# Prompt attention with part of the scaling on GpSimd, masks in fp32r, keys split in two parts, and two gathers moved by one stage

## The reference, cut to what matters

```python
N_HEADS, N_KV_HEADS, HEAD_DIM = 8, 2, 64       # 4 query heads to each key head
o_c, imp = cmp_attend(q, ckv, pos)             # 16 compressed keys, from compress(kvc)
idx, valid = select_blocks(imp, pos)           # 16 blocks of 64 keys: with 1024 keys, all of them
o_s = sel_prompt(q_rot, pos, idx, valid, kvs)  # so this is causal attention over all earlier keys
o_w = window_prompt(q_rot, kvw)                # the last 512 keys, by another set of keys and values
attn = g[:, :, 0] * o_c + g[:, :, 1] * o_s + g[:, :, 2] * o_w   # gates, per position and head
```

## Time and profile before

| | us |
|---|---|
| median of 3 runs | 1815.67 (1811.49 to 1818.6) |
| the profiled execution | 1816.98 |
| its span in the profile | 1814.5 |
| stage of keys ends, compression begins | at 379.3 |
| prompt attention, 128 steps | 529.8 to 815.5, its first maximum at 544.0 |

### The profile page before, as it was taken

How to read it: one execution, slowest core, us unless ns; L and a number is a source line. 1 busy time by engine, 2 the same in 40 slices (tenths; PEclk the granted TensorE clock), 3 DMA queues, 4 the chain that set the end, 5 groups by cost and what they waited for, 6 DMA issues and landing times. The chain is left out here.

```text
span 1814.5 us, 29420 instructions
## 1 busy us (share of the span) xinstructions
PE 1686.8 (93%) x11053; PEld 1490.5 (82%) x11053; DVE 949.3 (52%) x1625; ACT 756.4 (42%) x1233; POOL 340.3 (19%) x360
## 2 busy tenths in 40 slices
PE   6999979969979998998779999999999999999997
PEld 3888955558866777775569999999999999999997
DVE  3747672234457787774466644443444443444443
ACT  3435511124446576672233555432345332354322
POOL 1100051511020010021036404004213023100032
PEclk7999989978878999997889999999999999999999
DMA  8355320063502000104544444534544545445343
GB/s 298 106 151 173 102 75 24 0 222 125 179 5 93 2 1 1 53 2 198 235 121 131 128 139 133 145 112 129 154 134 139 150 123 156 141 134 161 113 141 96
DMA packets 296946, 214.36 MB, mean 118 GB/s; under 512 B 20293, under 2 KB 284277, under 8 KB 293590
## 3 DMA queue, kind: packets, MB, share of 16 engines
q1 hardware_dynamic: 290340, 176.51, 32.8%
q0 software_dynamic: 4672, 36.56, 5.3%
q10 hardware_dynamic: 1842, 0.05, 0.1%
HBM read 205.81 MB, written 11.41 MB: 120 GB/s over the span
## 5 line engine op out<-in xcount | busy, mean ns | idle before, releaser
L423 DVE TENSOR_TENSOR ff_lo<-ff_raw,ff_hi 128x2048 fp32r<-128x2048 f32 (+1 forms) x126 | 267.2, 2121 | 201.3 <-ACT ff_hi L419 201.2
L428 PE MATMUL banks<-low_rows,ff_hi 128*128 128x352 f32 x1120 | 359.2, 321 | 0.0
L427 PE MATMUL banks<-ff_h_hi,ff_hi 128*128 128x352 f32 x1056 | 341.7, 324 | 1.0 <-DVE ff_lo L423 0.9
L429 PE MATMUL banks<-ff_h_hi,ff_lo 128*128 128x352 f32 x1056 | 339.1, 321 | 0.0
L419 ACT ACTIVATE ff_hi<-ff_raw 128x2048 fp32r<-128x2048 f32 (+1 forms) x126 | 215.4, 1710 | 229.7 <-PE banks L429 220.0
L428 PEld LDWEIGHTS banks<-low_rows,ff_hi 128*128 128x128 f32 x1120 | 210.8, 188 | 0.3
L427 PEld LDWEIGHTS banks<-ff_h_hi,ff_hi 128*128 128x128 f32 x1056 | 198.1, 188 | 2.0 <-issue 1.8
L429 PEld LDWEIGHTS banks<-ff_h_hi,ff_lo 128*128 128x128 f32 x1056 | 198.2, 188 | 0.0
L427 PE MATMUL banks<-hid_hi,ff_hi 128*128 128x352 f32 x528 | 171.2, 324 | 4.3 <-DVE hid_lo L423 4.1
L429 PE MATMUL banks<-hid_hi,ff_lo 128*128 128x352 f32 x528 | 169.8, 322 | 0.0
L428 PE MATMUL banks<-hid_lo,ff_hi 128*128 128x352 f32 x528 | 169.4, 321 | 0.0
(11 more groups left out here) (435 smaller groups left out, 3231.3 us busy)
## 6 DMA issues: line engine op xcount, KB each, us to landing
ff_raw<-in_w_gate SPq DMA_DIRECT2D x66, 512.0 KB, 3.8
ff_raw<-in_w_up SPq DMA_DIRECT2D x66, 512.0 KB, 5.1
ff_raw<-in_w_down SPq DMA_DIRECT2D x48, 384.0 KB, 3.9
late_ada<-in_w_ada SPq DMA_DIRECT2D x16, 1024.0 KB, 5.5
ff_raw<-in_w_down SPq DMA_DIRECT2D x48, 320.0 KB, 3.2
ff_raw<-in_w_out SPq DMA_DIRECT2D x24, 512.0 KB, 4.5
s_raw<-in_w_in SPq DMA_DIRECT2D x48, 128.0 KB
streams<-in_x_prompt SPq DMA_DIRECT2D x4, 1024.0 KB, 9.2
```

The lines of the kernel that those rows point to most:

```text
L423: return dve.tensor_tensor(lo, raw, hi.bitcast(F32), ALU.subtract)
L427: pe.matmul(out, lhsT=w_hi, rhs=x_hi, start=first, stop=False)
L428: pe.matmul(out, lhsT=w_hi, rhs=x_lo, start=False, stop=False)
L429: return pe.matmul(out, lhsT=w_lo, rhs=x_hi, start=False, stop=last)
```

## The change

1. Stage of keys: POOL issues two gathers (part 0) before its last pair instead of four; those of part 1 are issued by POOL at the start of the stage of compression.
2. Weighing of branch 2 (64 of 128 steps) is shared: DVE makes the reciprocal only and counts `coef_ready`; POOL multiplies by reciprocal and gate. Semaphore `scaled` becomes `scaled_v` and `scaled_p`. POOL's other work in the stage (copies for `q_plain` and `q_rot`, squares) stands between these products.
3. Masks and the identity beside them are fp32r instead of bf16.
4. The first split of keys covers 2 tiles of 8 (256 of 1024 keys); the rest is split by ACT behind the first doubling of queries, and by DVE in round 1. PE waits for the rest before step 8.
5. Half of `q_lo` is cleared by POOL instead of DVE, and PE starts the compressed scores of trip 0 before it waits for the masks.

```diff
@@ keys_and_values, gpsimd
                         pool.wait_ge(nat_summed, T9)
-                        for n in range(2):
-                            for half in range(SG):
-                                load_past(pool, d, hT[:, :, :].rearrange("p k r -> p (k r)"), page_rows, half, n, rows_loaded)
+                        for half in range(SG):
+                            load_past(pool, d, hT[:, :, :].rearrange("p k r -> p (k r)"), page_rows, half, 0, rows_loaded)
@@ compress, gpsimd
-            for n in range(2, N_LCH):
-                pool.wait_ge(multiplied, (n - 1) * STEPS + AHEAD)
+            for n in range(1, N_LCH):
+                if n >= 2:
+                    pool.wait_ge(multiplied, (n - 1) * STEPS + AHEAD)
@@ prompt_attention
+    HEAD_TILES, REST_AT = 2, 1
+    KEY_PARTS = [slice(0, HEAD_TILES * P), slice(HEAD_TILES * P, SEQ)]
-        diag_b, tail_b, ident_b = [sb(nc, st, n, [P, P], mybir.dt.bfloat16) for n in ("diag_b", "tail_b", "ident_b")]
+        diag_b, tail_b, ident_b = [sb(nc, st, n, [P, P], F32R) for n in ("diag_r", "tail_r", "ident_r")]
+        def wait_scaled(eng, n):
+            _, _, br, h = order[n]
+            eng.wait_ge(scaled_v if br == 1 else scaled_p, n // 4 * 2 + h + 1)
@@ gpsimd
+            for h in range(N_KV):
+                pool.memset(QL[h][own[1 - h], :].bitcast(F32), 0.0).then_inc(q_clear, 1)
+                pool.wait_ge(q_clear, h + 1)
             pool.memset(vx, 0.0).then_inc(v_clear, 1)
...
+            steps = spread()
+            for n in range(N + 12):
+                if n < N and order[n][2] == 2:
+                    w, j = len(tiles_of[n]) * P, slice(n % 4, n % 4 + 1)
+                    pool.wait_ge(coef_ready, n // 4 * 2 + order[n][3] + 1)
+                    pool.tensor_scalar(probs[n % 3][:, 0:w], probs[n % 3][:, 0:w], coef[:, j],
+                                       gsel[order[n][0] % 2][:, order[n][1], 2, order[n][3]:order[n][3] + 1], ALU.mult, ALU.mult).then_inc(scaled_p, 1)
+                    pool.wait_ge(scaled_p, n // 4 * 2 + order[n][3] + 1)
+                if n >= 10 and n % 4 == 2 and (n - 10) // 4 // TILES in (1, KA - 1):
+                    square((n - 10) // 4)
+                if n < PER:
+                    next(steps, None)
@@ tensor
             def qk(n):
+                if n == HEAD_TILES * PER // TILES:
+                    pe.wait_ge(k_lo_done, 2 * N_KV)
...
             def turn(n):
-                pe.wait_ge(scaled, n + 1)
+                wait_scaled(pe, n)
...
+            pe.wait_ge(ck_ready, 1)
+            compress_scores(0)
             pe.wait_ge(masks_cast, 3)
-            compress_scores(0)
+            pe.wait_ge(q_clear, N_KV)
@@ scalar
-            for h in range(N_KV):
-                split_hi(act, KS[h][own[h], :, :], kT[own[h], :, 0:SEQ]).then_inc(k_hi_done, 1)
-            double(0, 0)
+            for part in KEY_PARTS:
+                for h in range(N_KV):
+                    split_hi(act, KS[h][own[h], :, part], kT[own[h], :, part]).then_inc(k_hi_done, 1)
+                if part is KEY_PARTS[0]:
+                    double(0, 0)
@@ vector, weigh(n)
-                s.then(dve.reciprocal(coef[:, j], den[:, j]))
-                dve.tensor_scalar(probs[n % 3][:, 0:w], probs[n % 3][:, 0:w], coef[:, j], gsel[i % 2][:, t, br, h:h + 1],
-                                  ALU.mult, ALU.mult).then_inc(scaled, 1)
+                if br == 2:
+                    if n >= 4:
+                        wait_scaled(dve, n - 4)
+                    dve.reciprocal(coef[:, j], den[:, j]).then_inc(coef_ready, 1)
+                else:
+                    s.then(dve.reciprocal(coef[:, j], den[:, j]))
+                    dve.tensor_scalar(probs[n % 3][:, 0:w], probs[n % 3][:, 0:w], coef[:, j], gsel[i % 2][:, t, br, h:h + 1],
+                                      ALU.mult, ALU.mult).then_inc(scaled_v, 1)
@@ vector, the rounds
+                if n == REST_AT:
+                    split_keys(1)
```

More of the change, by code:

```diff
@@ L1359, in prompt_attention @@
         acc = take_space(SEQ)
+        sq = take_space(P)
         diag, tail = probs[0][:, 0:P], probs[0][:, P:2 * P]
@@ L1429, in _, with spread @@
-            s.fence()
-            s = Steps(pool, pool_stepped)
[L1432 to L1443, removed]
-                            r.then_inc(squared, 1)
-                            pool.wait_ge(squared, t + 1)
-                        else:
-                            s.then(r)
+            def spread():
+                s = Steps(pool, queries_spread)
+                s.then(pool.memset(q_plain[:, :, :], 0.0))
+                s.then(pool.memset(q_rot[:, :, :], 0.0))
+                for b in range(BT):
+                    for h in range(N_KV):
+                        part = slice(h * HEAD_DIM, (h + 1) * HEAD_DIM)
+                        c0 = b * QR + h * DEC_SEQ * GROUP
+                        for dst, src in ((q_plain, qT), (q_rot, qR)):
+                            for g in range(SG):
+                                row = SEQ + (g * BT + b) * DEC_SEQ
+                                s.then(pool.tensor_copy(
+                                    dst[part, g * BT + b, c0:c0 + DEC_SEQ * GROUP].rearrange("p (s g) -> p s g", g=GROUP),
+                                    src[part, :, row:row + DEC_SEQ].rearrange("p g s -> p s g")))
+                                yield
@@ new lines, in _, with square @@
+            s = Steps(pool, pool_stepped)
+            def square(tile):
+                i, t = tile // TILES, tile % TILES
+                pool.wait_ge(taken, (tile + 1) * N_KV)
+                rows = slice(t * P, (t + 1) * P)
+                for n, c in enumerate((i // 2, 2 + i // 2)):
+                    x = attnT[:, c, rows]
+                    if i == 1 and n == 0:
+                        s.then(pool.tensor_tensor(acc[:, rows], x, x, ALU.mult))
+                        continue
+                    s.then(pool.tensor_tensor(sq[:, :], x, x, ALU.mult))
+                    r = pool.tensor_tensor(acc[:, rows], acc[:, rows], sq[:, :], ALU.add)
+                    if i == KA - 1 and n:
+                        r.then_inc(squared, 1)
+                        pool.wait_ge(squared, t + 1)
+                    else:
+                        s.then(r)
@@ L1449, in _ @@
+            for _ in steps:
+                pass
+            pool.wait_ge(scaled_p, N // 2)
         @block.tensor
@@ L1685, in weigh, with split_keys @@
                 dve.wait_ge(probs_ready, n + 1)
[L1686 to L1688 removed]
+                if br == 2:
+                    if n >= 4:
+                        wait_scaled(dve, n - 4)
+                    dve.reciprocal(coef[:, j], den[:, j]).then_inc(coef_ready, 1)
+                else:
+                    s.then(dve.reciprocal(coef[:, j], den[:, j]))
+                    dve.tensor_scalar(probs[n % 3][:, 0:w], probs[n % 3][:, 0:w], coef[:, j], gsel[i % 2][:, t, br, h:h + 1],
+                                      ALU.mult, ALU.mult).then_inc(scaled_v, 1)
             s.then(dve.memset(ck_pair[:, :, :], 0.0))
             for h in range(N_KV):
[L1692 removed]
                 s.done(dve.tensor_scalar(ck_pair[own[h], h, :], ck_p[own[h], :], SCALE, None, ALU.mult))
             s.fence()
+            dve.sem_inc(ck_ready, 1)
+            stage(0, 0)
+            def split_keys(part):
+                for h in range(N_KV):
+                    dve.wait_ge(k_hi_done, part * N_KV + h + 1)
+                    keys = KEY_PARTS[part]
+                    split_lo(dve, KS[h][own[1 - h], :, keys], kT[own[h], :, keys], KS[h][own[h], :, keys]).then_inc(k_lo_done, 1)
+            split_keys(0)
             dve.wait_ge(masks_loaded, 48)
@@ L1697, in _ @@
                 dve.tensor_copy(dst[:, :], src[:, :]).then_inc(masks_cast, 1)
-            stage(0, 0)
-            for h in range(N_KV):
-                dve.wait_ge(k_hi_done, h + 1)
-                split_lo(dve, KS[h][own[1 - h], :, :], kT[own[h], :, 0:SEQ], KS[h][own[h], :, :]).then_inc(k_lo_done, 1)
             compress_shift(0)
```

22 lines of the change are left out of this document (4 added, 18 removed).

## The result

The changed kernel took 1793.2 us (1792.1 to 1795.7, 4 runs) beside 1813.9 us of the kernel before on the same chip: ratio 0.9885, 95% interval 0.986 to 0.991. Run a second time beside others it took 1795.4 us, ratio 0.990 (0.988 to 0.992).

A forecast was written before the change was run, and what follows sets the result against it. TensorE was taken to bound most of prompt attention, with DVE next; the terms -5.3 - 1.5 - 4 - 2 + 1.5 + 1 + 3.5 summed to -6.8 us, giving 1809 us, the forecast's own range 1803 to 1815.

The forecast's parts named there:

- gathers: End of the stage of keys: it waits for four gathers to land; issuing two instead saves 5.3 us.
- start: Start of prompt attention: fewer fills and a shorter first split on DVE gain 1.5 us at the maximum at 552.85.
- branch 2 off DVE, t = 5 to 7: Tiles bound by PE: without DVE's product the copy of bank 5 comes earlier and PE's waits end, 4 us less.
- tiles t = 1: Tiles t = 1 of trips 0 to 2, bounded by DVE: three products leave it in each, 2 of 3.3 us gained.
- POOL: DVE's products, L1627: POOL's products hold DVE's own product and, in tiles t = 4 of trips 0 to 2, DVE's L1627: 1.5 us lost.
- POOL: squares: Trips 1 and 3: four squares between a tile's two POOL products make the second late in small tiles, 1 us lost.
- masks fp32r: 160 mask matmuls on PE: 0.04 us more each, 6.4 us, just over half on the path, 3.5 us lost.
- I take 1.9: POOL's product by two columns on 128x640, shown in no row: 1.2 or 2.1 us by proportion, taken as 1.9 us.
- A: Rival, chance 0.23: POOL's product takes 1.2 us so nothing collides, and masks cost nothing; 1803 us, range 1797 to 1807.
- B: Rival, chance 0.12: fp32r masks of 128 columns take 0.22 us, all on PE's path; 1829 us, or 1825.
- C: Rival, chance 0.13: POOL becomes the bound in trips 1 and 3 and blocks DVE; 1820 us.
- D: Rival, chance 0.05: the stage of keys doesn't end on the gathers, or the moved ones are waited for; 1814 us.

The follow-up runs named there:

- pool_twice: The changed kernel with each of POOL's 64 products done twice, the same piece first multiplied by 1 and 1 in place: 1802.2 us, ratio 0.993.

## Why the prediction was wrong

By its terms, in us; measured in the traces where rows give it:

```
term                              forecast (bounds)      measured
gathers                           -5.3 (-6.5..-4.8)      -5.0, -5.8
start                             -1.5 (-4..+1)          -3.0
branch 2 off DVE, t = 5 to 7      -4   (-6.4..-3.1)      -5.8 (6.2 less 0.4 of the masks)
tiles t = 1                       -2   (-3.3..0)         -1.6
POOL: DVE's products, L1627       +1.5 (-2..+5)          none seen in the tiles
POOL: squares                     +1   (0..+7)           0
masks fp32r                       +3.5 (0..+24)          -0.65
sum                               -6.8                   -16 to -17
```

**The failed step** is the side of costs. I put 6 us against the gains for masks and POOL; they cost nothing, and the masks even gained 0.65. For the masks "just over half on the path: 3.5 us" was drawn from a transpose's 0.11 us between starts, the wrong neighbour: the fp32r mask's distance to the next matmul is 0.13 us at 765.88 above, where the bf16 mask had 0.12 in the earlier trace rows. My lower bound of 0 excluded the gain without a reason. For POOL "I take 1.9" lay above the truth by a factor of two, and 0.89 lies below both of my ends (1.2 and 2.1). The slope is (894 - 453) / 512 = 0.86 ns a column. (The Trainium skill's "roughly line-rate", GPSIMD Engine Reference, section 4.1, would have been a better guide than the one-column product of the earlier trace rows.) pool_twice shows that with 1.75 us a loss would have come, in the small tiles with squares and in the tiles t = 4 that I named.

**The gains** were mis-sized the other way. The split keys gave 3.0 and not 1.5. I had the first maximum 2.5 us earlier and 1 us of that lost again to the rest of the split in round 1; it came 3.1 earlier and 0.1 was lost, since VectorE had idled for as long as the rest of the split takes (3.45 beside 3.54 us). In the large tiles I read the earlier trace rows alone. The direction and the mechanism were right (the product before the copy, "this wait of 0.26 us ends"), but the 6.4 us of PE's row were not all: the weight loads waited 13.6 us for the copy and 5.7 for the product, and the gain came out near my upper end. The matmuls' waits for kT, which I had expected to be gone, were 3.0 us in 3. The gathers were right.

**The rivals.** A came nearest (POOL cheap, masks free), and even its 1803 was too high by 8 to 10 and its range ended at 1797. B, C and D fell: no mask cost, trips 1 and 3 not longer than trip 2, the stage ends on the gathers. What I had in none: that the gain hangs on where the copy stands, and that moving the product took only a part of it. The copy still waits for the product of branch 1 in every second turn, and that is the 4.3 us that exchanging two lines takes out of the changed kernel's large tiles.

The measured terms don't close on the times: 16 to 17 us against 18 to 21. The rest, some 1 to 5 us, has no shown cause. The parts of the program that the change doesn't touch differ by several us between executions (from the last maximum to the end 997.4 to 1006.8 us, the stage of compression 146 to 151 us), so single traces can't place it.

## What to carry to other kernels

In a list that one engine works off in order, look at what stands in front of the instruction that frees a single bank: in the large tiles exchanging two neighbours was worth 10.0 us and moving 64 products to an idle engine 5.9, and load behind the copy cost nothing there. With the copy first, the kernel took 1791.9 us without the moved products and 1790.9 with them. Read the waits of the weight loads beside those of the matmuls; the first meet a wait that the second hide. For an operation that no row shows, don't let the doubtful side carry the forecast: here three cost terms that came out at nothing took 6 us off the gain. And before a stage's length in a single trace is put down to the change, lay the granted clock beside it.

## What the runs showed of the hardware

- POOL's product by two columns: 0.45 us at 128 columns, 0.55 at 256, 0.71 at 384, 0.77 at 512, 0.89 at 640 (groups of the profile after), while the one-column product of the earlier trace rows takes 1.16 at 352.
- Two VectorE products of 16 columns last 1.78 us beside POOL's two fills and 0.31 without; the rows above show both.
- The fp32r mask of 128 columns, between 4-byte matmuls, costs TensorE no more than the bf16 one: 0.13 us to the next start beside 0.12, and 0.6 to 0.7 us less in 23 tiles.
- The untouched work of the stage of compression takes 146.8 us at a mean granted clock of 0.88 and 150.6 at 0.85, both with four gathers in front of it.
- The tile t = 2 takes 5.67 us in trip 1 and 8.03 in trip 2 of the same execution, at mean granted clocks of 0.97 and 0.62 of full speed; 0.62 lies between the engine's two levels of 1.2 and 2.4 GHz. In front of both stands t = 1, in which VectorE is the bound; in trip 1 it was that tile which ran at the lower clock (0.78). Most of what single profiles differ by in the trips is this: the changed kernel run again has 5.89 us in place of 8.03, and its trips are 2.3 us shorter.

```profile
607.42:614.26 6.84, 5.19 (x29) 3.80 (x28) 5.69 (x22) 4.11 (x15) 0.85 (x2) 0.78 0.00 0
614.26:619.93 5.67, 5.42 (x43) 4.34 (x42) 3.79 (x12) 4.63 (x14) 1.15 (x3) 0.97 0.01 1
...
680.20:688.20 8.00, 7.34 (x41) 6.27 (x42) 3.98 (x13) 4.86 (x16) 2.98 (x6) 0.62 0.00 1
```
